# The transpose of a merged 64x64 inverse: 128x128 transposes in place of a third merge product

## The reference, cut to what matters

```python
def step(state, inp):
    r_t, w_t, k_t, v_t, a_t, b_t = inp
    sa = jnp.einsum('bhij,bhj->bhi', state, a_t)
    state = (state * w_t[:, :, None, :] + sa[..., None] * b_t[:, :, None, :]
             + v_t[..., None] * k_t[:, :, None, :])
    return state, jnp.einsum('bhij,bhj->bhi', state, r_t)
...
_, y = lax.scan(step, state0, (tm(rh), tm(heads(jnp.exp(log_w))), tm(kh), tm(vh), tm(a_vec), tm(b_vec)))
```

## Time and profile before

| | us |
|---|---|
| median of three runs (lowest, highest) | 3448.07 (3445.08, 3450.1) |
| profiled execution, its own time | 3445.68 |
| profiled execution, span from first to last instruction | 3443.9 |
| PE busy, DVE busy, ACT busy in the span | 3291.7, 1837.5, 1226.3 |
| first stage of `rwkv`, layer 1 and layer 2 | 53.3, 53.9 |
| second stage of `rwkv`, layer 1 and layer 2 | 38.9, 33.7 |

### The profile page before, as it was taken

The page is one execution under the profiler, slowest core; times in us unless marked ns, Lnnn a source line. Parts: engine busy times, 40 slices in busy tenths (PEclk is TensorE's granted clock), DMA queues, the critical chain, the costliest instruction groups (busy, mean ns, idle before and its releaser), DMA issues. The chain is left out here.

```text
span 3443.9 us, 48916 instructions
## 1 busy us (share of the span) xinstructions
PE 3291.7 (96%) x21306; PEld 2689.9 (78%) x21306; DVE 1837.5 (53%) x2575; ACT 1226.3 (36%) x1726; POOL 8.3 (0%) x8
## 2 busy tenths in 40 slices
PE   7999999799999999999998899999999989999997
PEld 5888886778788888888876778788887758778886
DVE  4434575555453445444675464443456776457475
ACT  3323445233332233223455143322243184344242
POOL 0000000000000000000000000000000000000000
PEclk9999999989999999999999999999999999999999
DMA  3323223023122232323221033232323203223231
GB/s 125 108 86 108 77 81 107 4 74 129 63 97 98 98 98 92 104 92 106 76 81 43 4 110 110 68 103 93 100 95 117 86 26 109 87 83 105 88 105 67
DMA packets 78197, 301.69 MB, mean 88 GB/s; under 512 B 8946, under 2 KB 9586, under 8 KB 77344
## 3 DMA queue, kind: packets, MB, share of 16 engines
q1 hardware_dynamic: 77984, 298.56, 26.2%
HBM read 296.40 MB, written 6.06 MB: 88 GB/s over the span
## 5 line engine op out<-in xcount | busy, mean ns | idle before, releaser
L323 DVE TENSOR_TENSOR w_lo<-ring,w_hi 128x1024 fp32r<-128x1024 f32 (+1 forms) x508 | 652.7, 1286 | 506.9 <-ACT w_hi L316 506.5
L341 PE MATMUL ps<-xa_hi,w_hi 128*128 128x512 f32 x1728 | 689.2, 399 | 15.5 <-DVE w_lo L323 13.5
L342 PE MATMUL ps<-xa_lo,w_hi 128*128 128x512 f32 x1728 | 678.8, 393 | 0.0
L343 PE MATMUL ps<-xa_hi,w_lo 128*128 128x512 f32 x1728 | 678.6, 393 | 0.0
L316 ACT ACTIVATE w_hi<-ring 128x1024 fp32r<-128x1024 f32 (+1 forms) x508 | 555.3, 1099 | 341.7 <-DMA ring<-in_ffn_in_dram 73.6
L341 PE MATMUL ps<-xb_hi,w_hi 128*128 128x512 f32 x1248 | 489.8, 392 | 0.0
L343 PE MATMUL ps<-xb_hi,w_lo 128*128 128x512 f32 x1248 | 486.1, 390 | 0.0
L342 PE MATMUL ps<-xb_lo,w_hi 128*128 128x512 f32 x1248 | 486.0, 389 | 0.0
L341 PEld LDWEIGHTS ps<-xa_hi,w_hi 128*128 128x128 f32 x1728 | 327.7, 190 | 98.8 <-DVE w_lo L323 15.0
L343 PEld LDWEIGHTS ps<-xa_hi,w_lo 128*128 128x128 f32 x1728 | 327.8, 190 | 69.2
L342 PEld LDWEIGHTS ps<-xa_lo,w_hi 128*128 128x128 f32 x1728 | 327.9, 190 | 68.8 <-issue 2.6
(11 more groups left out here) (373 smaller groups left out, 3306.2 us busy)
## 6 DMA issues: line engine op xcount, KB each, us to landing
ring<-in_ffn_in_dram SPq DMA_DIRECT2D x176, 512.0 KB, 3.4
ring<-in_ffn_out_dram SPq DMA_DIRECT2D x64, 704.0 KB, 4.1
ring<-in_mix_in_dram SPq DMA_DIRECT2D x58, 512.0 KB, 3.4
ring<-in_up_dram SPq DMA_DIRECT2D x44, 512.0 KB, 3.4
ring<-in_w_in_dram SPq DMA_DIRECT2D x22, 512.0 KB, 3.5
ring<-in_down_dram SPq DMA_DIRECT2D x16, 704.0 KB, 4.1
ring<-in_mix_out_dram SPq DMA_DIRECT2D x16, 512.0 KB, 4.2
ring<-in_xk_dram SPq DMA_DIRECT2D x16, 512.0 KB, 3.4
```

Source lines behind the costliest of these rows:

```text
L323: dve.tensor_tensor(core.w_lo[j][:, 0:width], core.ring[j][:, 0:width], core.w_hi[j][:, 0:width].bitcast(F32), ALU.subtract).then_inc(self ...
L341: pe.matmul(out, hi, x_hi, start=(opens and k == tiles[0]), stop=False)
L342: pe.matmul(out, hi, x_lo, start=False, stop=False)
L343: last = pe.matmul(out, lo, x_hi, start=False, stop=(closes and k == tiles[-1]))
```

## The change

`inv_t` is no longer merged by products. After a level has merged `inv`, PE transposes it with 12 transposes of 128x128 in the next level (four 64x64 systems each: two by rows, two by columns). For that the columns of `inv` and `inv_t` are laid out by pairs (`by_pair`). ACT copies the half of the columns that this level filled from PSUM to `inv_t`, in two operations of 512 and 256 columns. V of level n now waits for these copies (`took_tt`). The adds of V into `inv` become four DVE operations where two were. K moves: none in level 0, two in levels 1 to 4. In the last level the eight products with the unit matrix bring the whole old transpose to PSUM, so that the result is copied by DVE and ACT into a buffer of its own (`final_t`). No DMA is added, moved or removed.

The diff on PE:

```diff
...
-        inv_of = lambda h, r, n12: inv[half(r), col(h ^ r, n12)]
-        inv_t_of = lambda h, r, n12: inv_t[half(r ^ h), col(h, n12)]
+        by_pair = lambda w, n12: slice((2 * n12 + w) * C, (2 * n12 + w + 1) * C)
+        inv_of = lambda h, r, n12: inv[half(r), by_pair(h ^ r, n12)]
+        inv_t_of = lambda h, r, n12: inv_t[half(r ^ h), by_pair(r, n12)]
...
+        turned_of = lambda g: inv_t[:, groups[g][0] * P:groups[g][1] * P]
+        turned_in = lambda bank, g: ps[:, bank + 2 * g:bank + 2, :].rearrange("p b t -> p (b t)") if g == 0 else ps[:, bank + 2, :]
...
-                        pe.wait_ge(took_v, 2 * (n - 1) + g + 1)
+                        pe.wait_ge(took_v, 4 * (n - 1) + 2 * g + 2)
...
                     last.then_inc(made_x, 1)
                 pe.wait_ge(blank, n + 1)
                 if n:
-                    pe.wait_ge(took_tt, 2 * n)
-                    pe.wait_ge(masked_k, 4 * n)
+                    if n >= 2:
+                        pe.wait_ge(masked_k, 4 * n - 4)
+                    with_k(2 * n - 2)
+                    for lo, hi in groups:
+                        for n12 in range(lo, hi):
+                            at_n = n12 % 4 * P
+                            last = pe.transpose(ps[:, there + n12 // 4, at_n:at_n + P], inv[:, n12 * P:(n12 + 1) * P],
+                                                core.c("ident"))
+                        last.then_inc(made_tt, 1)
                 else:
                     pe.wait_ge(inverse_t, 2)
                 if more:
                     for g, (lo, hi) in enumerate(groups):
+                        if n:
+                            pe.wait_ge(took_tt, 2 * (n - 1) + g + 1)
+                            if g:
+                                pe.wait_ge(masked_k, 4 * n - 2)
                         pe.wait_ge(took_x, 2 * n + g + 1)
...
                         last.then_inc(made_v, 1)
-                    with_k(2 * n)
-                    for lo, hi in parts_t:
-                        for n24 in range(lo, hi):
-                            h, n12 = divmod(n24, 12)
-                            bank, cols = at(here, n24)
-                            for r in range(2):
-                                last = pe.matmul(ps[half(r ^ h), bank, cols], x_of(x, h, r, n12), inv_t_of(h, r, n12), start=True,
-                                                 stop=True)
-                        last.then_inc(made_tt, 1)
-                    pe.wait_ge(masked_k, 4 * n + 2)
-                    with_k(2 * n + 1)
+                    if n:
+                        with_k(2 * n - 1)
                 else:
-                    for r in range(2):
-                        for j, (lo, hi) in enumerate(groups):
-                            pe.matmul(ps[half(r), there + 2 + j, 0:(hi - lo) * C], core.c("eye")[half(1 - r), :],
-                                      inv_t[half(1 - r), U3 // 2 + lo * C:U3 // 2 + hi * C], start=True, stop=False)
+                    pe.wait_ge(took_tt, 2 * n)
+                    pe.wait_ge(masked_k, 4 * n - 2)
+                    for j, (lo, hi) in enumerate(groups):
+                        for h, r in ((0, 0), (0, 1), (1, 1), (1, 0)):
+                            pe.matmul(ps[half(r), there + 2 * h + j, 0:(hi - lo) * C].rearrange("p (n t) -> p n t", t=C),
+                                      core.c("eye")[half(r ^ h), :],
+                                      inv_t[half(r ^ h), :].rearrange("p (n r t) -> p r n t", r=2, t=C)[:, r, lo:hi],
+                                      start=True, stop=False)
                     for g, (lo, hi) in enumerate(groups):
                         pe.wait_ge(took_x, 2 * n + g + 1)
                         for n12 in range(lo, hi):
                             for h, r in ((0, 0), (0, 1), (1, 1), (1, 0)):
                                 bank, cols = at(there + 2 * h, n12)
-                                last = pe.matmul(ps[half(r), bank, cols], x_of(x, h, r, n12), inv_t_of(h, r, n12), start=(h == 0),
-                                                 stop=(h == 0 or n12 == hi - 1))
+                                last = pe.matmul(ps[half(r), bank, cols], x_of(x, h, r, n12), inv_t_of(h, r, n12), start=False,
+                                                 stop=(n12 == hi - 1))
                     last.then_inc(made_tt, 2)
+                    with_k(2 * n - 1)
```

ACT and DVE:

```diff
...
             for n, size in enumerate(sizes):
                 if n >= 2:
-                    act.wait_ge(made_tt, 2 * (n - 1))
+                    for g in range(2):
+                        act.wait_ge(made_tt, 2 * (n - 2) + g + 1)
+                        act.activation(columns(turned_of(g), 1, sizes[n - 2]), columns(turned_in(base(n), g), 1, sizes[n - 2]),
+                                       ACT.Copy).then_inc(took_tt, 1)
+                    act.wait_ge(made_v, 2 * (n - 1))
                 zeros = core.c("eye")[:, 0:1].unsqueeze(1).to_broadcast([P, U3 // 2 // size, size])
                 act.activation(columns(xs[n % 2], 1, size), zeros, ACT.Copy, scale=0.0).then_inc(blank, 1)
+            for g in range(2):
+                act.wait_ge(made_tt, 2 * (n_merge - 2) + g + 1)
+                act.activation(columns(turned_of(g), 1, sizes[-2]), columns(turned_in(base(n_merge), g), 1, sizes[-2]),
+                               ACT.Copy).then_inc(took_tt, 1)
             act.wait_ge(made_tt, 2 * n_merge)
-            act.activation(of_head(inv_t, 1), row(base(n_merge) + 2, 0, 12), ACT.Copy).then_inc(took_tt, 1)
+            act.activation(of_head(final_t, 1), row(base(n_merge) + 2, 0, 12), ACT.Copy).then_inc(took_tt, 1)
...
                                       ALU.mult).then_inc(took_x, 1)
+                if n:
+                    with_k(2 * n - 2)
                 if more:
                     for g in range(2):
                         dve.wait_ge(made_v, 2 * n + g + 1)
-                        to = cut(both(inv, g), 0, size)
-                        dve.tensor_tensor(to, to, cut(two_banks(there, g), 0, size), ALU.add).then_inc(took_v, 1)
-                    with_k(2 * n)
-                    for g, (lo, hi) in enumerate(parts_t):
-                        dve.wait_ge(made_tt, 2 * n + g + 1)
-                        to = columns(inv_t[:, lo * C:hi * C], 1, size)
-                        dve.tensor_tensor(to, to, columns(row(here, lo, hi), 1, size), ALU.add).then_inc(took_tt, 1)
-                    with_k(2 * n + 1)
+                        to, more_of = cut(pairs(inv, g), 0, size), cut(two_banks(there, g), 0, size)
+                        for w in range(2):
+                            dve.tensor_tensor(to[:, w], to[:, w], more_of[:, w], ALU.add).then_inc(took_v, 1)
+                    if n:
+                        with_k(2 * n - 1)
                 else:
                     dve.wait_ge(made_tt, 2 * n_merge)
-                    to = columns(of_head(inv_t, 0), 1, size)
-                    dve.tensor_tensor(to, to, columns(row(there, 0, 12), 1, size), ALU.add).then_inc(took_tt, 1)
+                    dve.tensor_copy(of_head(final_t, 0), row(there, 0, 12)).then_inc(took_tt, 1)
+                    with_k(2 * n - 1)
```

More of the change, by code:

```diff
@@ L2205, in rwkv @@
     xs = [a[6], a[7]]
+    final_t = xs[1]
     with stage(nc, "made", "masked", "made_i", "inverse", "made_it", "inverse_t", "eyed", "blank", "made_x", "took_x",
@@ L2213, in rwkv @@
         made_pair = lambda w, q: ps[:, 2 * q:2 * q + 2, 0:384].rearrange("p h (m w t) -> p w h m t", m=3, w=2)[:, w]
-        groups, parts_t = ((0, 8), (8, 12)), ((0, 16), (16, 24))
+        groups = (0, 8), (8, 12)
         base = lambda n: 4 * (n % 2)
@@ L2228, in rwkv @@
         of_head = lambda t, h: t[:, h * U3 // 2:(h + 1) * U3 // 2]
+        k_bank = lambda n: base((n + 1) // 2) + 3
+        turned_of = lambda g: inv_t[:, groups[g][0] * P:groups[g][1] * P]
+        turned_in = lambda bank, g: ps[:, bank + 2 * g:bank + 2, :].rearrange("p b t -> p (b t)") if g == 0 else ps[:, bank + 2, :]
         cut = lambda a, side, size: a.rearrange("p r n (k s t) -> p r n k s t", s=2, t=size)[:, :, :, :, side]
@@ L2235, in with_k @@
                 q, h = divmod(n, 2)
-                bank = base(n // 2) + 3
+                bank = k_bank(n)
                 for m in range(3):
@@ L2263, in _ @@
                 for h, r in CORNERS:
-                    bank, cols = at(4 + 2 * h, n12)
+                    bank, cols = at(4 + 2 * r, n12)
                     last = pe.matmul(ps[half(r ^ h), bank, cols], chunks(b_hat)[half(h), m, 2 * q + r, :],
@@ L2342, in with_k @@
                     dve.tensor_tensor(place(buf)[:, 4 * h + q],
-                                      ps[:, base(n // 2) + 3, 0:384].rearrange("p (m w t) -> p w m t", m=3, w=2)[:, w],
+                                      ps[:, k_bank(n), 0:384].rearrange("p (m w t) -> p w m t", m=3, w=2)[:, w],
                                       core.c(mask).unsqueeze(1).to_broadcast([P, 3, C]), ALU.mult).then_inc(masked_k, 1)
@@ L2353, in _ @@
```

(12 more changed lines are left out.)

1 line of the change is left out of this document (added).

## The result

| | before | changed |
|---|---|---|
| median of five runs each, us | 3448.07 | 3428.18 |
| lowest to highest, us | 3439.72 to 3450.16 | 3424.0 to 3430.51 |
| profiled execution, own time, us | 3445.68 | 3424.87 |

The ratio is 0.9944, with a 95% interval of 0.9929 to 0.996: some 14 to 24 us less. The forecast was 3428.0 us.

The account below looks back on a forecast made before the run. The prediction took the first stage to be bound by PE's code supply, 3.87 us per 256 instructions. Layer 1 -13.5 and layer 2 -6.6 gave -20.1 us, from 3448.07 to 3428 us, range 3421 to 3440.

Parts of the forecast that it names:

- Code as the bound of the first stage: First stage, both layers: PE waits for code in blocks of 256 instructions, 3.87 us each; 656 fewer instructions a layer.
- Layer 1, first stage: 2264 instructions left after the edge at 626.52 us, 34.2 us of code: -9.3, and +0.7 at the stage's end.
- So code stays the bound everywhere, narrowly at the end: First stage, changed kernel: each level's code outlasts its chain of waits; last level 7.4 us of code against 7.2.
- the end, for which I charged 0.7 us: End of the first stage: DVE's copy and last mask, 1.53 us, replace ACT's copy of 0.81; +0.7 in each layer.
- Layer 2, first stage: 2314 instructions left after the moved edge, 35.0 us of code: -7.3, with +0.7 for the end -6.6.
- I let PE enter it at the same time: Layer 2, first stage: the edge moved from 614 to 502 instructions in is entered at the old edge's time, 1902.00 us.
- Layer 1, second stage: The edge leaves the loop over chunks: PE reaches the loop 0.9 us later, the loop gains 5.8.
- The loop's -5.8: Loop over chunks, layer 1: without a gap it runs at 2.4 GHz as in layer 2; 14.06 us becomes 8.22.
- A: Rival: layer 1's loop over chunks stays at 1.2 GHz, no -5.8; -14.3, 3433.8 us; chance 0.22.
- B: Rival: gaps do not follow instruction count, only PE's own work counts; -4.5 a layer, 3439 us; chance 0.10.
- C: Rival: transposes do not keep the clock up, first-stage work takes twice its time; +21, 3469 us; chance 0.04.
- D: Rival: first stage's transpose, copy and adds between V and V become the bound; -9, 3439 us; chance 0.10.

Follow-up runs that it names:

- t_quads: Kernel before, with 32 of T's 48 products (the merge of `inv_t`) per level sent to four quadrants in turn, same instruction count; 3441.33 us.
- work_only: Changed kernel plus three unread products of 512 columns (12 instructions) at the end of levels 0 to 3; 3456.03 us.
- code_back_64: Changed kernel plus 41 unread products of 64 columns at the end of levels 0 to 3, 656 instructions a layer; 3450.56 us.
- k_late_2: Changed kernel with K behind the transposes in levels 1 to 3, last level one K ahead and one behind; 3427.5 us, ratio 0.9947.
- k_late: Changed kernel with K behind the transposes in levels 1 to 4, last level's second K ahead of the unit matrix; 3427.08 us, ratio 0.9944.
- code_back: Changed kernel plus 41 unread products of one column at the end of levels 0 to 3, 656 instructions a layer; 3464.33 us.

## Why the prediction was right

**Code as the bound of the first stage: right.** Work taken away leaves the stage as it is (t_quads), work added is half swallowed (work_only), and the instructions put back with the clock held restore the old length (code_back_64). The price per block, 3.87 us, was 3.83 and 3.72 in the changed kernel. The Trainium skill (Runtime: NRT & Kernel Launch, "Instruction fetch mechanics") calls the crossing of an edge mostly hidden. These runs disagree, with gaps of up to 1.9 us at edges, where the records between two edges are quick 64x64 products.

**Layer 1, first stage: -8.6 forecast (-9.3 and +0.7), -8.2 measured.** Two steps failed and nearly cancelled. "So code stays the bound everywhere, narrowly at the end" does not hold in the last level: after the edge at 649.94 us 736 instructions are left, 2.9 blocks or 11.1 us of code, but they took 12.0, without a gap by "issue" and with 0.77 us of waits for ACT's copies. There PE's own work and its waits are the bound. The prediction's own rows said so: its chain of 7.2 us left out the level's second K, while the 7.4 us of code have it in; with the 0.4 us of a K the chain is 7.6, above the code. And the end, for which I charged 0.7 us, costs nothing. DVE's timeline there:

```profile
661.37 0.96 DVE L2405 COPY big<-ps 128x768 f32<-128x768 f32 x1 [4.31 <-PE ps L2330]
662.25 0.61 DVE L2363 TENSOR_TENSOR scr<-ps,const 128x192 f32<-128x192 f32 x2
```

The copy begins while PE still works at the last K (661.13 to 661.96 us). DVE ends 0.90 us behind PE's last product, where ACT ended 0.89 behind it before.

**Layer 2, first stage: -6.6 forecast, -8.6 measured.** The step that failed is "I let PE enter it at the same time". The new edge, 500 instructions into the stage, ended its gap 7.72 us after the stage's start (1878.80 to 1886.52), the old one 9.77 (1892.23 to 1902.00). About 1.0 us of this is the clock. The first 96 records took 5.14 us, up to the start of the next group, in the profiled execution of before, at a granted clock of 0.50, and 4.11 now, at 0.63. The rows of before:

```profile
1892.23 5.40 PE L2247 MATMUL ps<-big 64*64 64x128 f32 x96 [3.90 <-PEq L119]
1897.37 1.99 PE L2256 MATMUL ps<-big 64*64 64x64 f32 x96
```

The second profile of the kernel before has 4.04 us there, so this part belongs to one execution. The rest is the 57 records by which the new edge comes earlier. From the edge on it took 35.7 us where I had 35.0, and the end cost nothing where I had 0.7.

**Layer 1, second stage: -4.9 forecast, -5.3 measured in this pair of profiles.** The loop did run as in layer 2 (9.36 us for 17.04), with no gap in it. That is 7.7 us, not 5.8: I had counted from the loop's second step on and left out the first, in which the gap of 1.64 us stood. The stage ahead of the loop paid 2.4 us (23.83 for 21.38), more than my 0.9, so the two errors nearly cancelled. PE's timeline of the changed kernel shows why it paid more:

```profile
685.12 2.66 PE L2490 MATMUL ps<-scr,big 64*64 64x64 f32 x92
...
688.98 0.73 PE L2500 MATMUL ps<-spare,scr 64*64 64x64 f32 x12
```

92 records took 2.66 us ahead of the loop, where 90 at the full clock take 1.55: the clock fell there (0.58 in the mean from 684.90 to 687.60 us), and was back before the loop's second step. In the second pair of profiles the loop gave 2.0 us and the way to it cost 3.5, 1.5 of them in the stage's first 96 records at a lower clock, so that this stage became 1.6 us longer.

**How much of the exact hit is luck.** The loop's -5.8 came from one execution of the kernel before; the second profile of it lost no such time. From the table, the four stages together changed by -22.1 us in the first pair of profiles and by -12.5 in the second. The medians differ by 19.9, the interval covers 14 to 24. The code term is in every pair: 8.2 and 8.6 us in the first, 8.6 and 4.7 in the second, 7.5 in the mean for each first stage, where I had 7.6. The term of layer 1's second stage is not: -5.3 in the first pair and +1.6 in the second, where I had -4.9. The loop's 5.8 should have been weighed by how often the clock falls, five times in seven by the counts above and once in two in the kernel before itself; I put it in whole. That the sum still met the median within 0.2 us is chance.

**The rivals.** *A*: the loop was fast in both profiles of the changed kernel; that it can fail is seen in k_late_2. *B*: excluded by the three runs named above; the first stages gained 7.5 us in the mean, not 4.5. *C*: the granted clock in the stage is 0.96 and 0.97, with 48 transposes in it. The Trainium skill (TensorE: Matmul & The Clock Gate, "Part 4: PE-mode transpose") has the full clock not engage for transposes. Here twelve took 1.53 us, 128 ns each, at a granted clock of 1.00 (635.76 to 637.29 us). *D*: the waits for copies are there, 0.25 to 0.28 us a level and 0.52 in the last, but in layer 2 they mostly took from the gaps at the edges, as k_late shows. That the last level pays for them follows from its having no gap in layer 1; how much of the 1 to 2 us that k_late gained there is theirs, no run separates.

**A size that was off without harm.** I expected gaps by "issue" of about 1.5 us; in layer 1 they are 0.8 to 1.0. The waits for ACT and DVE, which I had put at less, and the transposes stand in the same blocks and leave less to wait for.

## What to carry to other kernels

Where an engine shows idle time by "issue" at even distances, count the instructions between these gaps: if the number is the same each time, suspect that the stage is bound by how fast its code comes, and put in instructions and work separately to see which one costs time. Where it is the code, doing the same in fewer instructions gains until the work and its waits become the bound. In such a stage, shortening the work or moving waits buys little until the code is shorter; check at its last part, where the code in hand may suffice and the old rules hold again. And a term read from one execution, above all one on the clock, should be weighed by how often it occurs before it goes into a sum whole.

## What was not expected of the hardware

- **The clock in code_back.** Two kernels that differ only in the width of 164 added products a layer, 1 column or 64, had a granted clock of 0.83 and 0.81 in the first stages with the one and 0.97 and 0.94 with the other, and 59.2 and 60.2 us for 52.6 and 55.7. So filling instructions are not neutral: what is put in to test the count of instructions can change the clock.
- **The supply is not quite even.** Where nothing else stood in the way, a block took 3.60 us (ten blocks in layer 1 of code_back_64), 3.72 and 3.83 (the changed kernel), 3.87 (before). The first stage of the kernel before, with the same code, lasted between 50.0 and 53.9 us.
- **The fall of the clock in the loop is a matter of the execution**: after the same gap of 1.64 us at the same place it fell once and held once.
